# Run-up products on TensorE, operands that land late used last, and other places for turned pair outputs in a two-block transformer kernel

## What is computed

```
h = x
h = h + rmsnorm(gmlp(rmsnorm(h)))          # boundary 0 ahead of it
h = h + rmsnorm(conv_ffn(rmsnorm(h)))      # boundary 1
h = h + rmsnorm(diff_attention(rmsnorm(h)))# boundary 2
h = h + rmsnorm(conv_ffn(rmsnorm(h)))      # boundary 3
h = h + 0.5 * swiglu(rmsnorm(h))           # boundary 4
h = h + cat(mla, moba)(rmsnorm(h) @ w_in) @ w_out   # boundary 5 ("MIX")
h = h + 0.5 * swiglu(rmsnorm(h))           # boundary 6
out = rmsnorm(h)
rmsnorm(x) = x * rsqrt(mean(x*x) + EPS) * gain
```

## Time and profile before

| what | value |
|---|---|
| median of 3 runs | 1075.33 us (1075.19 to 1076.16) |
| profiled execution: time / span | 1076.43 us / 1074.6 us |
| TensorE products busy | 1054.8 us, 98% of the span |
| VectorE / ScalarE busy | 776.3 us (72%) / 654.5 us (61%) |
| DMA moved | 198.14 MB, 184 GB/s in the mean |
| granted TensorE clock, mean | 0.998 |

### The profile page before, as it was taken

The page is one execution under the profiler, slowest core; times in us unless marked ns, Lnnn a source line. Parts: engine busy times, 40 slices in busy tenths (PEclk is TensorE's granted clock), DMA queues, the critical chain, the costliest instruction groups (busy, mean ns, idle before and its releaser), DMA issues.

```text
span 1074.6 us, 15598 instructions
## 1 busy us (share of the span) xinstructions
PE 1054.8 (98%) x5944; PEld 911.8 (85%) x5944; DVE 776.3 (72%) x1229; ACT 654.5 (61%) x1176; POOL 36.4 (3%) x38
## 2 busy tenths in 40 slices
PE   7999999999999999999999999999999999999997
PEld 5987888888799878888887888888899988888886
DVE  5888988878767889878887755665676857566554
ACT  6767765567657778566667645545556657454454
POOL 0830000000000000000000000000000000000000
PEclk9999999999999999999999999999999999999999
DMA  9763766565463347666554765567345525656651
GB/s 356 229 232 125 252 202 204 186 203 185 171 220 106 111 150 245 194 198 194 183 189 135 239 197 193 177 195 215 129 163 161 197 59 181 211 176 196 190 183 40
DMA packets 56779, 198.14 MB, mean 184 GB/s; under 512 B 6577, under 2 KB 8537, under 8 KB 56705
## 3 DMA queue, kind: packets, MB, share of 16 engines
q1 hardware_dynamic: 56448, 196.94, 56.2%
q0 software_dynamic: 112, 0.20, 0.1%
q10 hardware_dynamic: 144, 0.00, 0.0%
HBM read 195.35 MB, written 1.25 MB: 183 GB/s over the span
## 4 chain that ended last, share of the span: by engine, by line
PE 93%; DVE 4%; ACT 2%; issue 1%; DMA 0%; SPq 0%; ACTq 0%
PE G L1407 27%; PE Y L1465 25%; PE G L1411 14%; PE G L1392 3%; PE G L1393 3%; PE G L1394 3%; PE G L1442 2%; PE G L1443 2%; PE G L1448 2%; PE Y L1460 1%; DVE w_low L855 1%; PE Y L1393 1%; PE Y L1392 1%; PE Y L1394 1%; PE G L1590 1%; PE Y L1473 1%
## 5 line engine op out<-in xcount | busy, mean ns | idle before, releaser
L855 DVE TENSOR_TENSOR w_low<-raw,w_high 128x1024 fp32r<-128x1024 f32 x352 | 425.0, 1225 | 37.4 <-ACT w_high L442 35.7
L442 ACT CAST w_high<-raw 128x1024 fp32r<-128x1024 f32 x352 | 363.8, 1046 | 10.8 <-DMA raw<-in_panels 10.8
L1407 PE MATMUL G<-x_parts,w_high 128*128 128x512 f32 x1280 | 319.6, 392 | 0.0
L1407 PEld LDWEIGHTS G<-x_parts,w_high 128*128 128x128 f32 x1280 | 234.1, 188 | 44.7
L529 ACT COPY big<-G 128x512 f32<-128x512 f32 x80 | 46.8, 585 | 237.9 <-PE G L1411 237.9
L1411 PEld LDWEIGHTS G<-x_parts,w_low 128*128 128x128 f32 x1280 | 174.6, 190 | 12.5
L1411 PE MATMUL G<-x_parts,w_low 128*128 128x256 f32 x1280 | 178.5, 282 | 0.0
L959 DVE TENSOR_TENSOR w<-G,big 128x512 f32<-128x512 f32 x80 | 55.3, 691 | 164.5 <-ACT big L529 164.3
L1465 PE MATMUL Y<-w_high,a_high 128*128 128x512 f32 x420 | 132.0, 395 | 1.1 <-DVE a_low L968 1.1
L1465 PE MATMUL Y<-w_high,a_low 128*128 128x512 f32 x420 | 130.1, 391 | 0.0
L1465 PE MATMUL Y<-w_low,a_high 128*128 128x512 f32 x420 | 129.7, 390 | 0.0
(11 more groups left out here) (246 smaller groups left out, 1185.1 us busy)
## 6 DMA issues: line engine op xcount, KB each, us to landing
raw<-in_panels SPq DMA_DIRECT2D x352, 512.0 KB, 4.3
gain_pre<-in_gains SPq DMA_DIRECT2D x7, 512.0 KB, 6.4
gain_post<-in_gains SPq DMA_DIRECT2D x4, 512.0 KB, 7.0
big<-in_xT SPq DMA_DIRECT2D x4, 256.0 KB, 7.3
h<-in_x SPq DMA_DIRECT2D x2, 512.0 KB, 8.4
big<-rel_rows SPq DMA_DIRECT2D x8, 128.0 KB, 5.0
out_y<-w SPq DMA_DIRECT2D x4, 256.0 KB, 2.2
big<-in_w_s SPq DMA_DIRECT2D x1, 512.0 KB, 10.0
```

The costliest lines, as they stand in the source:

```text
L442: s.copy(WH[:, n % RING, :], raw[:, n % RAWS, :]).then_inc(hi, 1)
L855: v.tensor_tensor(WL[:, n % RING, :], raw[:, n % RAWS, :], WH[:, n % RING, :].bitcast(F32), ALU.subtract).then_inc(lo, 1)
L1407: mm(out, WH[:, n % RING, k * P:(k + 1) * P], X2[:, k, :, :], start=k == 0, stop=False, skip_group_check=True)
```

## The change

It has eight parts.

1. `run_up`: 12 products of ones by ones (128x128, float32, into a PSUM bank that is used later) as TensorE's first work, and 4 more after the first block of x is scaled. Panel 0 is loaded on ScalarE's DMA queue, ahead of g0, and no longer on SyncE's.
2. h gets an extra column that holds sqrt(EPS * D); the square of the second half reads 513 columns, both squares are scaled by D ** -0.5, and ScalarE's root takes the first half's sum as its bias. `half_mean` goes.
3. Boundaries with a norm of their own: on VectorE `h_add(b, 1)` stands ahead of `x_low(b, 0, 2)` and the low split of panel base+3 behind both. The other boundaries: the splits of panel base+2 go ahead of the norm of tile 0 on both engines, and VectorE's of base+3 goes behind `h_plus_y(b, 1)`.
4. `last_values`: for tile 0 and the last two of the four panels, TensorE takes all products with x's high part first, then those with x's low part, and the products with the low part of panel base+3 last.
5. The last hidden block of a convolution stage: VectorE makes `hidden_low` of the block before between its two pairs of taps.
6. MIX, pairs 8 to 11: outputs are turned into a bank of Y (`pair_turned`), scores all go to the first two banks of Y, and `scores(9)` stands in the middle of `moba_pair(2)`.
7. MIX, pairs 12 to 15: `pair_out(a-1)` stands behind `weigh_values(a, 1)`, between the two halves of the rows; the split of panel base+3 of the next stage moves ahead of `cast(14)` (ScalarE) and `outs(15)` (VectorE); a `turn` of the first half waits for the first half of the exponentials only, and `cast(a-1)` stands between the halves of `exps(a+1)`.
8. The final store of the first half of the columns is issued by ScalarE.

```diff
-            load(0), load(1)
+            load(1)
...
+            act.dma_start(raw[:, 0, :], io["panels"][0]).then_inc(ld[0], 16)
             act.dma_start(g0[:], io["gain_first"]).then_inc(g0_in, 16)
...
+            run_up(12)
+            pe.wait_ge(x0h, 1)
+            run_up(4)
             value_panels(0, 0, (0, 1))
...
+                    cols = slice(c * 512, (c + 1) * 512 + c)
+                    s.activation((sqj if b else sqx)[:, t, cols], h[:, t, cols], ACT.Square, scale=D ** -0.5,
+                                 accum_out=ss2[:, t, c:c + 1]).then_inc(h_sq, 1)
+                act.wait_ge(h_sq, 4 * b + 2 * t + 2)
+                s.activation(sd2[:, t:t + 1], ss2[:, t, 1:2], ACT.Sqrt, bias=ss2[:, t, 0:1]).then_inc(h_std, 1)
...
                     y_gained(b, 1, 1)
+                    h_add(b, 1)
                     x_low(b, 0, 2)
-                    h_add(b, 1)
-                    half_mean(b, 1)
-                    upto(base + 3)
                 else:
                     h_plus_y(b, 0)
-                    half_mean(b, 0)
+                    upto(base + 2)
                     x_normed(b, 0)
-                    upto(base + 2)
                     x_low(b, 0, 0), x_low(b, 0, 1), x_low(b, 0, 2)
-                    upto(base + 3)
                     h_plus_y(b, 1)
-                    half_mean(b, 1)
+                upto(base + 3)
                 x_normed(b, 1)
...
+                both(0, WH, 2), both(0, WL, 2)
+                pe.wait_ge(hi, n + 2)
+                both(0, WH, 3)
+                pe.wait_ge(xl_r, part)
+                both(1, WH, 2), both(1, WH, 3)
+                ready(n + 1)
+                return both(0, WL, 3, True)
...
+                    if f == NF - 1:
+                        first_taps(f, lambda: hidden_low(ph, NF - 2))
+                        continue
...
+        def pair_turned(a):
+            return (Y[:, 2, :] if a < 11 else PB)[:, 0:T]
...
-            turn(8, 0), scores(9), turn(8, 1), weigh_values(8, 0), moba_pair(2), weigh_values(8, 1)
+            turn(8, 0)
+            moba_pair(2, lambda: (scores(9), turn(8, 1), weigh_values(8, 0)))
+            weigh_values(8, 1)
...
+                out_split(a - 11)
+                rows(B + 24 + a - 11, (a - 7) % KT, 0, False, False)
+                weigh_values(a, 1)
                 if a > 12:
                     pair_out(a - 1)
-                if a < 14:
-                    out_rows(a - 11)
-                weigh_values(a, 1)
-            out_rows(3)
+                rows(B + 24 + a - 11, (a - 7) % KT, 1, False, False)
```

More of the change, by code:

```diff
@@ L369, in _ @@
             for t in range(TT):
[L370 to L372 removed]
+                sp.wait_ge(out1_r, t + 1)
+                sp.dma_start(io["out"][tok(t), half(1)], xn[:, t, half(1)]).then_inc(out_sem, 16)
             sp.wait_ge(out_sem, 64)
@@ L462, in h_rms @@
             def h_rms(b, t):
-                for c, done in ((0, h_sq0), (1, h_sq1)):
+                for c in range(2):
                     if b:
@@ L598, in swiglu_ffn, with exps @@
                     share(f, base, 1)
-            def exps(a):
+            def exps(a, between=None):
                 b = a % 2
@@ L609, in exps @@
                                         accum_out=sm[:, b, 2 + m:3 + m])
+                    if m == 0:
+                        if a >= HEADS:
+                            last.then_inc(ex0_r, 1)
+                        if between is not None:
+                            between()
                 last.then_inc(ex_r, 1)
@@ L1449, in values, with last_values, both @@
                 return last
+            def last_values(b, n, out, t):
+                part = sixth(b, t, 2)
+                ready(n)
+                pe.wait_ge(xh_r, part)
+                def both(level, W_part, q, last=False):
+                    for k2 in range(2):
+                        k = 2 * q + k2
+                        end = mm(out, X2[:, k, level, tok(t)], W_part[:, (n + q - 2) % RING, half(k2)],
+                                 start=False, stop=last and k2 == 1)
+                    return end
+                both(0, WH, 2), both(0, WL, 2)
[5 more added lines that the diff above has]
+                return both(0, WL, 3, True)
             def rows(n, slot, t, first, last):
@@ L1508, in first_four @@
                 n = STARTS[b]
-                for p in range(4):
-                    last = values(b, n + p, p, out[0], 0)
+                for p in range(2):
+                    values(b, n + p, p, out[0], 0)
+                last = last_values(b, n + 2, out[0], 0)
                 if done is not None:
@@ L1609, in _, with run_up @@
             pe.wait_ge(consts, 1)
+            def run_up(n):
+                for _ in range(n):
+                    mm(Y[:, 0, 0:P], ones[:], ones[:], start=True, stop=True)
+            run_up(12)
+            pe.wait_ge(x0h, 1)
+            run_up(4)
             value_panels(0, 0, (0, 1))
@@ L1754, in moba_pair @@
                     tile_out(B + 10 + 2 * j + m, G[:, (j + 1) % 2, m * T:(m + 1) * T])
-                    if j == 1 and m == 0:
-                        column_factors()
+                    if m == 0 and between is not None:
+                        between()
             def mla_q(u):
```

90 lines of the change are left out of this document (38 added, 52 removed).

## The result

The forecast was 1069.2 us (1067.8 to 1071.9). Measured, ten runs each: **1078.80 us** (1077.53 to 1079.18) after, 1075.39 us (1075.14 to 1076.43) before; the ratio is 1.0029, with a 95% interval of 1.0020 to 1.0037. The change made the kernel slower by 3.4 us. The profiled execution of after took 1078.41 us, its span is 1076.5.

A forecast was written before the change was run, and what follows sets the result against it. TensorE, busy 98% of the span, was taken as the bound, so only its waits and slow clock could be won: 2.0 + 3.6 + 0.7 - 0.25 + 0.25 = 6.3, taken as 6.1, giving 1069.2 us (1067.8 to 1071.9).

The forecast's parts named there:

- The extra column costs one element in 513, nothing.: Square of the second half, reading h's added column: the longer read was put at no cost.
- The start: First products: dummies raise the clock early, g0 lands at 5.5, TensorE starts at 7.6; gain 2.0 us, bounds 0.3 and 2.4.
- g0 waits for SyncE's panel too: Rival at the start: g0 lands at 7.3, TensorE starts at 9.4, start gives 0.3; 1070.9 us, chance 0.16.
- the other rival: Clock stays slow: TensorE's pauses around the dummies lose the 2.5 of the clock; 1071.6 us, chance 0.12.
- The 2.5 for the clock: Start: twelve products and part of a thirteenth save 0.2 us each if the dummies raise the clock beforehand.
- The boundaries: Stage boundaries 1 to 6: reordered VectorE work and splits shorten TensorE's waits; gain 3.6 us, bounds 2.0 and 4.2.
- Boundary 3's term: Boundary 3, second token tile: earlier h_add and normed rows gain 0.7 us of a wait of 1.4.
- 0.7 turns into a wait at the first transposes of boundaries 2 and 4: Convolution's last block: its removed wait mostly returns at those transposes, leaving a gain of 0.1 us each.
- MIX, pairs 8 to 11: Moving scores(9) gains 0; pair_out in another bank need not wait for the turn's copy: 0.7 us, bounds 0.2 and 1.2.
- Pairs 12 to 15: MIX: waits go, but outs(15) and low_out(14) come 1.0 late behind a split; net cost 0.25 us, bounds -0.5 and +1.2.
- The stores: End of kernel: two store issues lie side by side, sharing DMA engines; gain 0.25 us, bounds 0 and 0.4.
- the one mechanism for slower: Rival: every split waits behind a late g0 on ScalarE, slower if g0 lands past 13.9; 1078 at 14.5, chance 0.03.

The follow-up runs named there:

- e1: Kernel before plus two unused 32-byte tensors (behind h and big2), so every tensor stands where the changed kernel has it: 1083.02 us, ratio 1.0072.
- e9: Changed kernel plus 992 unused bytes behind h and 992 behind big2, restoring TensorE's operand addresses modulo 1,024: 1070.72 us, ratio to before 0.9952.
- e4: Changed kernel with g0 issued ahead of panel 0 on ScalarE's queue: 1076.81 us.
- e12: Changed kernel with 992-byte pads behind h and big2, panel 0 back on SyncE's queue, pair 15's low split behind outs(15) and low_out(14): 1067.88 us.
- e16: As e12, but without the sixteen products of ones (the run-up): 1068.95 us.
- e3: Kernel before with only the 12 and 4 products of ones added, loads and order unchanged: 1075.24 us, ratio 0.9998.
- e5: Kernel before with one unused 128-byte tensor behind h, moving x_parts and all that follows by 128 bytes: 1085.10 us, ratio 1.0089.
- e6: Kernel before with 32 unused bytes ahead of a_high and 96 behind a_low, x_parts left in place: 1080.54 us, ratio 1.0046.
- e2_after_64: Changed kernel with two more unused 32-byte tensors, x_parts to big2 64 bytes and all behind 128 further than before: 1072.30 us, ratio to before 0.9972.

## Why the prediction was wrong

**The step that failed** is a term that was put at nothing, behind the stores: "The extra column costs one element in 513, nothing." Its instruction does cost nothing: in after the square of 513 columns takes 0.63 us, that of 512 too. But for the column two tensors were also made wider, and with them moved the operands of nearly every product. The forecast costed the instruction that reads the column and never asked what else the declaration changes. Its price is 1078.80 - 1070.72 = **8.1 us**. That is close to the 8.7 estimated above from the pitches, and to the 7.6 of e1. Without it the rest of the change gives 4.9, where 6.1 was forecast. That these two are near each other is in part luck: the start missed by 2.6 one way, the boundaries by 1.6 the other (5.2 for 3.6, below).

**The start** was forecast at -2.0 with g0 at 5.5. The rival "g0 waits for SyncE's panel too" had it at 7.3 and TensorE at 9.4, with a start that gives 0.3; measured are 7.46 and 9.75, and a start that loses: with the place mended (e9) boundary 1's first turn begins 0.6 later than in the trace before (83.91 for 83.28), since the clock's fall in the pause comes on top. That the dummies' pause can cost the clock was said under the other rival; the two came together, because it is the late g0 that makes the pause. The rule of the Trainium skill, "DMA: Bandwidth & Descriptors", section on queues, rings and completion order, by which this rival would hold, agrees with what came: g0 at 7.46 for 7.3. Panel 0 on the second queue was later, not sooner (its cast at 7.10 in e4, 5.68 in e12); with it back on SyncE's the start gives what it should (e12: first product at 6.77, panel 7's wait 0.56). The 2.5 for the clock was read from an execution in which it rose late (after thirteen products, where other traces with this start have six to thirteen); the run-up measured 1.1 (e16 against e12) and 0.2 (e3).

**The boundaries**, forecast 3.6, gave more. At the old pitch (e9) TensorE's starts are late by this much over their usual distance, before and in e9: boundary 1 1.4 and 0.6, boundary 2 with the convolution's end ahead of it 1.7 and 0.7, boundary 3 2.0 and 0.9, boundary 4 with its convolution 1.7 and 0.6, boundary 5 0.7 and 0. The differences (0.8, 1.0, 1.1, 1.1, 0.7) make 4.7, above the bound of 4.2. The waits went as described, but sizes were off. Boundary 3's term was 0.7 and is 1.1. And "0.7 turns into a wait at the first transposes of boundaries 2 and 4" was too dark: they come 0.35 late, not 0.6.

**MIX, pairs 8 to 11**: `scores(9)` no longer waits and `scores(10)` does (0.5), as said; three `pair_out`s lost 0.28 each. Forecast 0.7, measured 1.0 (e9). **Pairs 12 to 15**: `pair_out(15)` is 1.0 late for the split ahead of `outs(15)`, exactly as forecast:

```profile
871.54 1.23 DVE L868 TENSOR_TENSOR w_low<-raw,w_high 128x1024 fp32r<-128x1024 f32 x1 [3.43 <-ACT w_high L448]
...
872.68 0.85 DVE L1314 TENSOR_SCALAR otk<-G,rs 128x64 f32<-128x64 f32 x4
873.45 0.42 DVE L1322 TENSOR_TENSOR a_low<-G,a_high 128x256 fp32r<-128x256 f32 x1
874.02 0.41 PE L1848 MATMUL G<-cst,otk 128*128 128x128 f32 x2 [0.83 <-DVE a_low L1322]
```

`turn(14, 0)` and `turn(15, 0)` met no `low_out`, though, so the whole gave 0.1 (e9) and did not cost 0.25. With the split behind `low_out(14)` (e12) that wait is gone too. **The stores** lie side by side and end 0.1 earlier, within the bounds of 0 to 0.4.

The parts, 4.7 + 1.0 + 0.1 + 0.1 - 0.6 = 5.3, compare with 5.7 between the spans of before and e9 (1074.6 and 1068.9; the profiled execution of before was 1.0 above its median, hence 5.7 here and 4.9 there). Laid side by side product by product, the two traces close that gap: e9 is 0.6 late ahead of boundary 1 and 4.6 early behind boundary 5 (761.74 for 766.30), so the boundaries gave 5.2; the lead is 5.4 at the end of the pairs 8 to 11 (826.11 for 831.50), 5.6 in boundary 6 and 5.7 at the end. The chances (0.91 for faster) were too sure: no case held a cost outside of the waits, and the one mechanism for slower was again a wait.

What stays open is why distance matters. The loading of the next product's block and the streaming of the current one go on at the same time (PEld is busy for 85% of the span and PE for 99%), so a clash of the two reads would fit, but no run separates a product's own two operands from the next one's block, and none explains why 256 columns are fastest at 64.

## What to carry to other kernels

When a change makes a tensor wider, adds one or takes one away, read the addresses of what lies behind it before costing its instructions, and keep the two operands of the main products at the same address modulo 256 (or put the odd-sized tensor last); this is shown for the float32 products of this kernel only. Compare mean durations of the main products by form as well as the waits: a kernel can lose 8 us without one wait more. Work that holds a clock up is only worth having without a long pause behind it (2.6 us lost the clock here, 1.4 did not), so what it bridges to must not be made later by the same change.

## What the hardware showed that I had not expected

- Products of 128x512 in float32 with both operands at the same address modulo 256: median pitch 0.227 us; at a distance of 32, 64 or 128: 0.231 to 0.234. Products of 256 columns: 0.120 at 0, 0.117 at 32, 0.117 to 0.118 at 64, 0.119 at 128. In all up to 9.5 us of 1075 (e5). The Trainium skill, "SBUF — State Buffer", in the section on the bandwidth-pool intuition, gives TensorE a second, independent read port for loading weights; by that alone a distance between operands should make no difference, and the measurements say that it does (e1, e5, e6). They don't say that the two reads share a port.
- The granted clock fell to 0.50 in a pause of TensorE of 2.6 us and was back at 1.00 only at 11.0, 3 us after work had begun again. In a pause of 1.4 us (e2_after_64, and 1.45 in e4_g0_first) it stayed at 1.00, and the products behind were 0.23 to 0.25 apart.
- In the slow start of the kernel before the granted clock shows 1.00 while products are 0.43 apart, so there the pitch, not that column, tells the clock. The rise came after six products in one execution and thirteen in another. The row of before:

```profile
7.00:10.00 3.00, 2.81 (x7) 2.26 (x8) 2.80 (x4) 2.04 (x4) 0.00 (x0) 1.00 1.01 393
```
